# The causal mask of forgetting attention: added by TensorE as a matmul, or by VectorE from a second bias tile

## The reference, cut to what matters

```python
def forgetting_attention(q, k, v, f_logit):
    log_f = jax.nn.log_sigmoid(f_logit.astype(F32))
    cum = jnp.cumsum(log_f, axis=1).transpose(0, 2, 1)
    outs = []
    for blk in range(s // Q_BLOCK):              # Q_BLOCK = 128
        q0 = blk * Q_BLOCK
        q1 = q0 + Q_BLOCK
        logits = jnp.einsum('bihd,bjhd->bhij', q[:, q0:q1], k[:, :q1]).astype(F32) * d ** -0.5
        logits = logits + cum[:, :, q0:q1, None] - cum[:, :, None, :q1]
        mask = jnp.arange(q0, q1)[:, None] >= jnp.arange(q1)[None, :]
        p = jax.nn.softmax(jnp.where(mask, logits, -jnp.inf), axis=-1).astype(v.dtype)
        outs.append(jnp.einsum('bhij,bjhe->bihe', p, v[:, :q1]))
```

## Time and profile before

| | us |
|---|---|
| runs of the kernel, median of 3 | 2924.6 (2924.59 to 2924.82) |
| the profiled execution, its own time | 2922.77 |
| its span, first to last instruction | 2921.0 |
| TensorE busy | 2890.6 (99%) |
| VectorE, ScalarE, POOL busy | 1070.7, 1086.2, 1167.5 |
| granted TensorE clock over the span | 0.998 |
| stage of forgetting attention, layer 0 and layer 1 | 209 to 263, 1114 to 1168 |

### The profile page before, as it was taken

How to read it: one execution, slowest core, us unless ns; L and a number is a source line. 1 busy time by engine, 2 the same in 40 slices (tenths; PEclk the granted TensorE clock), 3 DMA queues, 4 the chain that set the end, 5 groups by cost and what they waited for, 6 DMA issues and landing times.

```text
span 2921.0 us, 36339 instructions
## 1 busy us (share of the span) xinstructions
PE 2890.6 (99%) x15431; PEld 2426.4 (83%) x15431; DVE 1070.7 (37%) x1791; ACT 1086.2 (37%) x1659; POOL 1167.5 (40%) x499
## 2 busy tenths in 40 slices
PE   8999999999999999999999999999999999999999
PEld 5888888888888888888898888988888977888888
DVE  6433582466664534322242210541110366521101
ACT  4335333343323424432343332443222366432222
POOL 2332344344444432344444444334444333244442
PEclk9999999999999999999999999999999999999999
DMA  8332363346564422333333333333333322233332
GB/s 258 114 85 66 108 188 107 89 156 197 188 196 143 108 57 60 87 94 94 101 88 100 94 96 97 91 91 100 97 94 98 94 69 73 73 97 98 95 95 77
DMA packets 529686, 315.08 MB, mean 108 GB/s; under 512 B 16210, under 2 KB 507380, under 8 KB 529268
## 3 DMA queue, kind: packets, MB, share of 16 engines
q1 hardware_dynamic: 529524, 312.75, 36.4%
HBM read 310.61 MB, written 2.10 MB: 107 GB/s over the span
## 4 chain that ended last, share of the span: by engine, by line
PE 95%; DVE 2%; ACT 1%; SPq 1%; DMA 0%; issue 0%; POOL 0%; ACTq 0%
PE b L434 22%; PE b L436 22%; PE b L435 22%; PE o L434 5%; PE o L435 5%; PE o L436 5%; PE b L477 1%; PE b L478 1%; PE b L479 1%; PE b L1020 1%; PE b L1021 1%; PE b L1022 1%; PE o L839 1%; PE s L722 1%; PE s L819 1%; DVE aP L2633 1%
## 5 line engine op out<-in xcount | busy, mean ns | idle before, releaser
L2776 POOL TENSOR_TENSOR lo<-raw,hi 128x1024 fp32r<-128x1024 f32 (+1 forms) x489 | 1165.3, 2391 | 1718.5 <-ACT hi L1281 1718.2
L434 PE MATMUL b<-HH,hi 128*128 128x512 f32 x1832 | 728.2, 398 | 0.8 <-ACT GT L1635 0.8
L436 PE MATMUL b<-HH,lo 128*128 128x512 f32 x1832 | 713.7, 390 | 0.0
L435 PE MATMUL b<-HL,hi 128*128 128x512 f32 x1832 | 713.5, 389 | 0.0
L1281 ACT ACTIVATE hi<-raw 128x1024 fp32r<-128x1024 f32 (+1 forms) x492 | 507.6, 1039 | 413.1 <-DMA raw<-in_w_down_dram 103.4
L434 PEld LDWEIGHTS b<-HH,hi 128*128 128x128 f32 x1832 | 343.8, 188 | 80.6 <-issue 7.2
L436 PEld LDWEIGHTS b<-HH,lo 128*128 128x128 f32 x1832 | 343.9, 188 | 73.1
L435 PEld LDWEIGHTS b<-HL,hi 128*128 128x128 f32 x1832 | 344.0, 188 | 72.8 <-issue 2.4
L434 PE MATMUL b<-FH,hi 128*128 128x512 f32 (+1 forms) x594 | 219.9, 370 | 0.0
L436 PE MATMUL b<-FH,lo 128*128 128x512 f32 (+1 forms) x594 | 219.4, 369 | 0.0
L435 PE MATMUL b<-FL,hi 128*128 128x512 f32 (+1 forms) x594 | 219.4, 369 | 0.0
(11 more groups left out here) (499 smaller groups left out, 4414.2 us busy)
## 6 DMA issues: line engine op xcount, KB each, us to landing
raw<-in_w_up_dram SPq DMA_DIRECT2D x88, 512.0 KB, 4.0
raw<-in_w_in_dram SPq DMA_DIRECT2D x80, 512.0 KB, 4.2
raw<-in_w_ada_dram SPq DMA_DIRECT2D x80, 512.0 KB, 5.0
raw<-in_w_mg_dram SPq DMA_DIRECT2D x48, 512.0 KB, 3.8
raw<-in_ffn_w_gate_dram SPq DMA_DIRECT2D x44, 512.0 KB, 3.8
raw<-in_ffn_w_up_dram SPq DMA_DIRECT2D x44, 512.0 KB, 3.8
raw<-in_w_down_dram SPq DMA_DIRECT2D x32, 512.0 KB, 3.9
raw<-in_ffn_w_down_dram SPq DMA_DIRECT2D x32, 512.0 KB, 3.8
```

What stands on the lines that cost most here:

```text
L434: e.matmul(out, wh, xh, start=start and k == 0, stop=False)
L435: e.matmul(out, wh, xl, start=False, stop=False)
L436: mm = e.matmul(out, wl, xh, start=False, stop=stop and k == last)
L2776: e.tensor_tensor(t["lo"][:, s, 0:w], K.raw[:, s, 0:w], t["hi"][:, s, 0:w].bitcast(F32), ALU.subtract).then_inc(*m.lo.up(n))
```

## The change

The product with `causalR` goes, and its two operands with their startup copies. In their place VectorE builds, once per head, a second bias tile `foxCM` (two buffers): CB minus the mask in each of its four 128-column blocks (`masked(h)`). `top` is split in two for i > 0: the columns before the diagonal block are added to CB and reduced into `foxM2`, the diagonal block is added to foxCM and reduced into `foxM`, and a `tensor_tensor` max of one column joins them. `masked` stands ahead of step 0 for head 0, and behind scale in steps 1, 7 and 11 for heads 1, 2 and 3.

```diff
@@ TensorE, score(n)
-            q.wait_ge(m.vattn.at("fn", l, h), m.vattn.at("fn", l, 4 + h), free[b], m.anorm.at("causalR"))
-            e.matmul(o[:, 0:w], t["fq"][:, h, i * 128:w], t["fk"][:, h, 0:w], start=True, stop=False)
-            e.matmul(o[:, i * 128:w], t["identR"][:, :], t["causalR"][:, :], start=False,
+            q.wait_ge(m.vattn.at("fn", l, h), m.vattn.at("fn", l, 4 + h), free[b])
+            e.matmul(o[:, 0:w], t["fq"][:, h, i * 128:w], t["fk"][:, h, 0:w], start=True,
                      stop=True).then_inc(*m.attn.up(("fs", l, n)))
@@ ScalarE, startup
-        e.activation(t["identR"][:, :], t["ident"], ACT.Copy).then_inc(*m.anorm.up(("identR",)))
-        e.activation(t["causalR"][:, :], t["causal"], ACT.Copy, scale=-1.0).then_inc(*m.anorm.up(("causalR",)))
@@ VectorE, fox_attention
+            d = w - 128
-            q.wait_ge(m.attn.at("fs", l, n), m.aattn.at("fc", l, h), m.attn.at("ft", l, n - 3) if n >= 3 else None)
-            e.tensor_tensor_reduce(P[:, n % 3, 0:w], bank[f"s{n % 2}"][:, 0:w], CB[h % 2][:, 0:w], 1.0, -3e38, ALU.add,
-                                   ALU.max, M[:, n:n + 1]).then_inc(*m.vattn.up(("fm", l, n)))
+            q.wait_ge(m.attn.at("fs", l, n), m.vattn.at("fcm", l, h), m.attn.at("ft", l, n - 3) if n >= 3 else None)
+            if i:
+                e.tensor_tensor_reduce(P[:, n % 3, 0:d], bank[f"s{n % 2}"][:, 0:d], CB[h % 2][:, 0:d], 1.0, -3e38, ALU.add,
+                                       ALU.max, t["foxM2"][:, n:n + 1]).then_inc(*m.vattn.up(("fmo", l, n)))
+            e.tensor_tensor_reduce(P[:, n % 3, d:w], bank[f"s{n % 2}"][:, d:w], t["foxCM"][:, h % 2, d:w], 1.0, -3e38,
+                                   ALU.add, ALU.max, M[:, n:n + 1]).then_inc(*m.vattn.up(("fm", l, n)))
             q.wait_ge(m.vattn.at("fm", l, n))
+            if i:
+                e.tensor_tensor(M[:, n:n + 1], M[:, n:n + 1], t["foxM2"][:, n:n + 1], ALU.max).then_inc(
+                    *m.vattn.up(("fmax", l, n)))
+                q.wait_ge(m.vattn.at("fmax", l, n))
             e.tensor_scalar(M[:, n:n + 1], M[:, n:n + 1], -1.0, None, ALU.mult).then_inc(*m.vattn.up(("fneg", l, n)))
+
+        def masked(h):
+            q.wait_ge(m.aattn.at("fc", l, h))
+            e.tensor_tensor(t["foxCM"][:, h % 2, :].rearrange("p (b c) -> p b c", b=4),
+                            CB[h % 2][:, :].rearrange("p (b c) -> p b c", b=4),
+                            t["causal"].unsqueeze(1).to_broadcast([128, 4, 128]), ALU.subtract).then_inc(
+                *m.vattn.up(("fcm", l, h)))
...
+        masked(0)
         for n in range(19):
             if n < 16:
                 top(n)
             if 1 <= n <= 16:
                 scale(n - 1)
+            if n in (1, 7, 11):
+                masked((n + 1) // 4 + (n == 1))
             if n >= 6 and n % 4 == 2:
                 value((n - 6) // 4)
@@ places
-        fixed("identR", [128, 128], F32R)
-        fixed("causalR", [128, 128], F32R)
+        fixed("foxM2", [128, 16])
...
+        area("foxCM", 8, [128, 2, S])
```

## The result

The changed kernel takes 2929.32 us (median of 20 runs, 2927.64 to 2931.61), the kernel before, on the same chip, 2924.48 (20 runs, 2922.72 to 2925.64). The ratio is 1.0019, 95% interval 1.0012 to 1.0025: 4.8 us slower, 0.17%, inside what was named as the bound of no change, and inside the range. The forecast of 2926.9 was 2.4 us short: +2.3 was forecast, and +4.8 measured. The profiled execution took 2929.24, with a span of 2927.4 at a mean granted clock of 0.997; the one before, 2922.77, 2921.0 and 0.998. The profiled pair is thus 6.5 us apart, 1.6 more than the medians.

The account below looks back on a forecast made before the run. TensorE, busy 99% of the span, was taken as the bound. Product savings, new waits and turn 8's freed wait came to +1.17 us per layer, +2.3 in all, on a median of 2924.6: 2926.9 us, range 2922.8 to 2931.0.

Parts of the forecast that it names:

- the rival of the lost race: Rival: VectorE's scaling of score 8 starts after POOL's second pair and is held; 2930.6 us, from 2929.9 to 2931.2; chance 0.26.
- The product's price: TensorE, forgetting attention: each mask product left out saves 0.07 us, 32 of them 2.24 us, all on the path.
- The split reduction: VectorE, i > 0: second half starts with the first's read; with the dependent max the chain grows 0.28 us.
- turns 6, 10 and 14: TensorE turns of those scores (head n // 4, block n % 4): new waits for scaling, 0.08, 0.08 and 0.30 us.
- Max 2 held, scale 1 behind POOL's second half: Step 2: POOL's first subtraction holds score 2's max, its second holds score 1's scaling; turn 1 starts 1.99 us later.
- the rival of a max that slips through: Rival: POOL doesn't hold the 128x1 max; step 2 loses nothing, -0.65 us per layer, 2923.3 us; chance 0.13.
- Scale 8's race: Step 8, VectorE against POOL: scaling of score 8 issued 0.10 us before POOL's second pair, formerly 0.10 late.
- turn 8 doesn't wait: Step 8, TensorE: the former 0.78 us wait goes, so the shift falls from +1.55 to +0.7 us.
- Bias 3: TensorE's bias product of head 3, behind EfL, which follows the held scaling of score 9: +1.15 us.
- POOL's second pair: POOL's later two subtractions in layer 0: start at 235.5, end at 240.2, moving 0.41 us later against TensorE.
- The lock's other half: Head 1's masked tile on VectorE also holds POOL's first pair: 0.2 to 0.4 us more per layer, 2927.5 us.

Follow-up runs that it names:

- the kernel with the product kept: Changed kernel with the mask product put back behind every score, startup copies back too: 2930.53 us, ratio 1.0024 to the kernel before.
- pointer form: Changed kernel with the max as a tensor_scalar taking foxM2 as per-partition scalar, negation still apart: 2923.96 us, ratio 0.9999 to the kernel before.
- the max alone: Kernel before, product and whole reduction kept, plus one 128x1 two-input max of foxM with itself for i > 0: 2929.60 us, ratio 1.0019.
- fused kernel: Changed kernel with max and negation in one tensor_scalar, run twice: 2921.73 and 2922.44 us, ratios 0.9993 and 0.9995 to the kernel before.
- the change twice: The changed kernel in its first measurement and again unchanged: 2929.32 and 2928.93 us, ratios 1.0019 and 1.0018 to the kernel before.
- the shifted one: Changed kernel with eight more bias products in layer 0, ahead of the stage: 2931.35 us, ratio 1.0027 to the kernel before.

## Why the prediction was right, and where it was short

The time alone would not have decided: 2929.32 lies nearer to the rival of the lost race (2929.9 at the least) than to the forecast of 2926.9. The trace decides, and it has the mechanism that was forecast, with a term too small and one missing.

- **The product's price** held: from score 8 to turn 6 it was 0.29, and from a 128-column score to the turn behind it it is now 0.22 (score 4 at 220.54, turn 2 at 220.76 after). The stages of the kernel with the product kept agree. By the Trainium skill's rule for a matmul ("VectorE: DVE Perf Modes", section on the TRN2 errata) that would have been an estimated 0.056; the distance of starts says 0.07. What was not seen is that the kernel before could not use all of it: with nothing else changed, only half arrives, since turn 2 then waits for a scaling held by POOL, and turn 8 waits longer for another.
- **The split reduction** held: the second half starts with the read of the first (212.41, 212.41), and turns 6, 10 and 14 come out near the forecast: score 8 to turn 6 is 0.30 now, the 0.22 without a product and the wait of 0.08 that was forecast, and turn 14 stands 0.27 later behind turn 13 than before, forecast 0.30.
- **Max 2 held, scale 1 behind POOL's second half** held to the hundredth: +2.00 for +1.99. The pointer form takes it away, the max alone brings it about; the rival of a max that slips through is out.
- **Scale 8's race** was won by 0.16 where 0.10 was forecast; that rival is out here, with the margin as thin as it was said to be.
- **The step that was mis-sized** is what comes after the won race: "turn 8 doesn't wait, and the shift falls from +1.55 by 0.07 and 0.78". Turn 8 did come early, at +0.80. But value 1, which stands 0.11 behind it where nothing waits, stands 0.73 behind: 0.62 of the 0.78 is lost again there, for ScalarE's copy of turn 7, which follows its weight pair. ScalarE in time, that copy before:

```profile
234.74 0.59 ACT L1542 ACTIVATE foxT<-t 128x512 f32<-128x512 f32 x1
```

  and from the weight pair to the copy after:

```profile
235.11 2.00 ACT L1280 ACTIVATE hi<-raw 128x1024 fp32r<-128x1024 f32 x2
237.01 0.50 ACT L1531 ACTIVATE foxP<-foxP,foxM 128x256 f32<-128x256 f32 x1
...
237.50 0.59 ACT L1539 ACTIVATE foxT<-t 128x512 f32<-128x512 f32 x1
```

  Before, the copy ended at 235.33, just in time for a turn 8 without its wait (at 235.22, value 1 0.11 later). Now it ends at 238.09, and value 1 starts at 238.14. The pair was at 24.77 after the first L809 before and is at 26.92: 2.15 later, where turn 6 is 1.66 later. I had moved POOL's pair by this difference (0.41 forecast, 0.49 measured), and not what ScalarE does next.

  Of this only a part reaches the end. Bias 3 comes at +1.47 for +1.15, and EfL ahead of it waits for two: EfH's copy, which hangs on value 1 and ends at 241.20, and scale 9, which ends at 241.08. So some 0.2 of the 0.32 is value 1's, and the rest is scale 9's, since POOL's second pair starts 28.06 after the first L809 and was forecast at 27.92. The term is +1.54 a layer for +1.17, 0.7 us in all.
- **The clock was not in the sum at all.** It is worth 1.5 us in layer 1, more than the mis-sized term.
- **The lock's other half shows too**, in POOL's first subtraction. POOL's two subtractions of layer 0's first pair (min/median/max ns; the first of the two is the shorter before and the longer in the others), before, after, and with the product kept:

```profile
L2776 POOL TENSOR_TENSOR lo<-raw,hi x2: 2394/2418/2442, 213.2 to 215.6; 128x1024 fp32r<-128x1024 f32 x2
L2791 POOL TENSOR_TENSOR lo<-raw,hi x2: 2344/2427/2510, 213.8 to 216.3; 128x1024 fp32r<-128x1024 f32 x2
L2794 POOL TENSOR_TENSOR lo<-raw,hi x2: 2347/2509/2671, 213.4 to 216.0; 128x1024 fp32r<-128x1024 f32 x2
```

  Where 0.12, 0.26, 0.32 and 0.43 us of the masked tile are left when POOL's first subtraction starts (fused kernel, change, pointer max, product kept), it takes 2.39, 2.51, 2.57 and 2.67; where no masked tile runs it takes 2.39. From the change on that is longer by what was left, less 0.14 or 0.15 each time. The Trainium skill ("SBUF — State Buffer", section "Who interferes with whom") has the engine that comes first block the other fully, and these rows agree. The 0.2 to 0.4 us that this would have added did not come, since the pair as a whole hardly grew, 4.81 for 4.79: its second subtraction takes 2.34 for 2.44, now that scale 1 no longer ends 0.16 inside it but is issued after its start. The same section's rule that VectorE doesn't contend with at most one SBUF input, outside its 2-port modes, agrees with the pointer max at 0.21.

By stages the change costs 1.54 + 1.54 and the clock 1.5, 4.6 in all, beside a measured 4.8. Of the 2.4 us that the forecast was short, the mis-sized term is 0.7 and the clock 1.5.

Open: why the clock falls behind one idle of some 2 us and not behind another of the same length. The fall in layer 1 was there in all four profiles with 2.0 us of idle or more (the change twice, the product kept, the shifted one) and in none of the eight others, the one with 1.74 among them; in layer 0 the same idle brought it only in the shifted kernel.

## What to carry to other kernels

Where an engine runs long two-input operations on SBUF beside VectorE, a one-column `tensor_tensor` on VectorE's chain costs what is left of the long one, not 0.15 us: give the second column as the pointer operand of a `tensor_scalar`, and fold the next operation into it. And before a wait is booked as given back, read what the same engine waits for next, and whether that moved too: here each kernel that freed turn 8 had also moved ScalarE's copy of turn 7, and value 1 waited for it.

## What was not expected of the hardware

- 2.0 to 2.2 us of idle on TensorE was followed, about 1 us after it resumed, by some 3 us at a granted clock of about half, at a cost of 1.45 to 1.5 us, in 5 of the 8 places (four profiles, two layers): there the idle costs 1.7 times its length. In layer 0 of the changed kernel the same idle cost nothing more; a shift by 1.95 us brought the fall there too.
- A fall of about the same size in block two (between 2432 and 2448, once near 2500) appears in some executions of a kernel and not in others (the fused kernel has one of each). By its size it may be what parts single runs of one kernel into two groups some 1.5 us apart; that was not tried.
- Two 128x1 operations of the same arithmetic, with the second operand as a tensor and as a pointer, took 1.40 and 0.21 us at the same place beside POOL's subtraction, and 0.16 for the first without it.
- VectorE's operation holds POOL as well: POOL's subtraction grew by what was left of a 128x512 `tensor_tensor` already running, less 0.14 or 0.15 us, in three kernels (2.51, 2.57 and 2.67 us for 2.39).
